# A hybrid retention and attention step on one core: first two units by token pieces, merge exponential before the stores, last down chunk split at token 896

## The chip, the core and the metric

The kernel runs on one core of a Trainium2 chip. The metric is the device time of one execution in microseconds (us), the median of several runs. Engines are named as in the profile: PE (TensorE matmul), PEld (its weight loads), DVE (VectorE), ACT (ScalarE), POOL (GpSimd) and SP (SyncE, which here only issues DMAs).

## What is computed

One inference step for 1024 prompt tokens and 8 sample tokens, 1032 in all, with a model width of 1024. Cut to what matters here:

```python
hn = rms_norm(x, norm_mix)
proj = hn @ w_in                      # rq, rk, rv, rg, aq, ak, av, gate_r, gate_a
ro = swish_gated(group_norm(retention(rq, rk, rv)))
outs, lses = three_dilated_attention_groups(aq, ak, av)
wgt = softmax(stack(lses), axis=0)    # the merge: three groups by their denominators
ao = einsum('gnth,gnthd->nthd', wgt, stack(outs))
merged = sigmoid(gate_r) * (ro @ w_ret) + sigmoid(gate_a) * (ao @ w_att)
x = x + merged @ w_out
hn = rms_norm(x, norm_ffn)
gate, up = split(hn @ w_gate_up)
x = x + (silu(gate) * up) @ w_down
y = rms_norm(x, norm_final)
```

Everything is float32. States, window buffers and new key/value rows are outputs too.

## The kernel before, in words

**Operands.** A product in float32 is made of three passes over operands that are split into a high part and a remainder: high weight by `a_hi`, high weight by `a_lo`, low weight by `a_hi`. All tokens lie transposed in `wide` (128 partitions, 8 rows of k, 1032 tokens); ACT makes `a_hi`, DVE makes `a_lo`. POOL splits each weight tile of `w_raw` into `w_part` with two instructions (L776, L778).

**Units.** A unit is one 128-column tile of a projection over all tokens: 8 steps of k, 3 passes, 3 pieces of 344 tokens, so 72 matmuls into `unit_ps[0]` or `unit_ps[1]`. `unit()` issues them (L896), and its argument `between` puts small tasks (transposes, attention tiles, sums) between the steps of k. A unit waits for its split weights (`w_split`) and until DVE has taken the unit two before from the same PSUM tile (`unit_free`). Splitting the weights of unit j waits until unit j-2 is done. Small tasks use the two banks `task_banks`; `task_done` and `task_free` hand them over. The order on every engine is written out by hand: each engine has one in-order stream.

**Head.** SP loads nine row tiles of x through a ring of four buffers (L543). PE transposes each, four 128x128 blocks to a bank (L934); DVE copies bank 0 and ACT bank 1 into `wide` (L1851, L1353). ACT squares each tile as well (L1361) for the norm. After the ninth tile ACT makes eight whole rows of `a_hi` (L1369), DVE eight of `a_lo` (L1860), and unit 0 follows the rows of `a_lo` as they come. ACT takes the square roots (L1372), DVE the reciprocals and a diagonal matrix `diag` (L1864 to L1869), and `x_norm(j)`, four small PE tasks (L943), spreads the factors over partitions. They stand before steps 0 to 3 of unit 1, and the first waits for `diag_ready`. DVE multiplies by `rstd` as it takes each unit (L1835).

**Merge.** Sixteen branch units begin at `U_BRANCH`; I call them branch unit 0, 1 and so on. `LATE_AT` places fourteen small tasks in them: entry j is (unit, step of k). Entries 0 to 5 and 10 to 13 are sample tasks, entries 6 to 9 the four merge tasks, which transpose `ao_tok` (L1184). `ao_tok` comes out of DVE: `merge_weights` (L2153 to L2173, with ACT's exponential L1627 in its middle), then `merge_group(0)`, `gated_branch(0)`, `merge_group(1)`, `gated_branch(1)`, `merge_group(2)`. Groups 1 and 2 are two 128x2048 instructions each (L2184, L2187). `gated_branch(m)` empties the PSUM tile of branch unit m (L2206).

**Tail.** The last chunk of the down projection runs twice over its 8 output tiles: `last_unit` for token pieces 0 and 1 (688 tokens, 8 x 42 matmuls of 344 columns, L1302), then for piece 2 (8 x 21). Between the latter, `turn_rows(t)` turns finished tiles of 128 tokens back into rows (L1311); ACT squares and takes the root (L1807, L1810), DVE scales (L2437), SP stores. `EARLY` = 688 makes five of nine tiles turn between units, and four after the last one.

Of the kernel before, what the change touches and what calls it, by code (L numbers as in the profile page):

```python
# [29 lines left out]
ALU = mybir.AluOpType  # L30
# [49 lines left out]
EARLY = 2 * PIECE  # L80
# [39 lines left out]
X_ROWS = 4  # L120
# [3 lines left out]
LATE_AT = ((0, 1), (0, 2), (0, 4), (0, 5), (0, 6), (0, 7), (2, 6), (2, 7), (3, 1), (3, 2), (4, 6), (5, 2), (5, 4), (5, 6))  # L124
# [114 lines left out]
def build(nc, a, out):  # L239
    ctx = ExitStack()  # L240
    with ctx:
# [31 lines left out]
        with ExitStack() as s:  # L273
            x_row = sb("x_row", [P, X_ROWS, D], stack=s)
# [113 lines left out]
        x_loaded = [sem(f"x_loaded{i}") for i in range(X_ROWS)]  # L388
# [4 lines left out]
        diag_ready = sem("diag_ready")  # L393
        a_high = sem("a_high")
# [134 lines left out]
        def _(sp):  # L529
# [5 lines left out]
            cols = (COL_RV, COL_RV + P, COL_RK, COL_RQ)  # L535
            for t in range(CHUNKS + 1):
                r = t % X_ROWS
                if t >= X_ROWS:

                    sp.wait_ge(task_done[1], t - X_ROWS + 1)  # L540
                    sp.wait_ge(squared, t - X_ROWS + 1)
                if t < CHUNKS:
                    sp.dma_start(x_row[:, r, :], a["x_prompt"][0, t * P:(t + 1) * P, :]).then_inc(x_loaded[r], 16)  # L543
                else:
                    sp.dma_start(x_row[0:SAMPLES, r, :], a["x_sample"][:, 0, :]).then_inc(x_loaded[r], 16)
                if t == X_ROWS:
                    load(Place(0), 0, KT, w_in[:, :, cols[0]:cols[0] + P])
            for j in range(1, 4):
                load(Place(0), j, KT, w_in[:, :, cols[j]:cols[j] + P])
# [328 lines left out]
        def _(pe):  # L878
# [48 lines left out]
            for t in range(CHUNKS + 1):  # L927
                rows = P if t < CHUNKS else SAMPLES
                pe.wait_ge(x_loaded[t % X_ROWS], 16 * (t // X_ROWS + 1))
                for b in range(2):  # L930
                    ps = begin(Place(0), 2 * t + b)
                    for q in range(4):
                        c = (4 * b + q) * P
                        mm = pe.transpose(ps[:, q * P:q * P + rows], x_row[0:rows, t % X_ROWS, c:c + P], ident[0:rows, 0:rows])  # L934
# [355 lines left out]
            def last_unit(pl, m, taken, ready=None):  # L1290

                s, nf = m % 2, FF_CHUNKS[LAST]
                hi, lo = h_rows(LAST)
                weights = w_part[:, m] if m < 2 else w_keep[:, m - 2]
                pe.wait_ge(w_split, U_LAST + m + 1)
                pe.wait_ge(unit_free[s], pl.half(m))
                for k in range(nf):
                    if ready:
                        pe.wait_ge(ready[0], ready[1] + k + 1)
                    for part, (w, x) in enumerate(((0, hi), (0, lo), (1, hi))):  # L1300
                        for n in taken:
                            mm = pe.matmul(unit_ps[s][:, n, 0:PIECE], weights[:, w, k, :], x[:, k, n * PIECE:(n + 1) * PIECE],  # L1302
                                           start=(k == 0 and part == 0), stop=(k == nf - 1 and part == 2))
                mm.then_inc(unit_done, 1)
# [25 lines left out]
        def _(act):  # L1330
# [24 lines left out]

            for t in range(CHUNKS + 1):
# [8 lines left out]
            for b in range(2):  # L1365
                act.wait_ge(task_free[b], CHUNKS + 1)
            act.wait_ge(gains_loaded, 16)
            for k in range(KT):
                act.activation(a_hi[:, k, :], wide[:, k, :], ACT.Copy, scale=gains[:, 0, k:k + 1]).then_inc(a_high, 1)  # L1369
# [256 lines left out]
            act.wait_ge(mrg_dve, 1)  # L1626
            act.activation(mrg[:, 0:3, :], mrg[:, 0:3, :], ACT.Exp).then_inc(mrg_act, 1)  # L1627
# [187 lines left out]
        def _(dve):  # L1815
# [33 lines left out]
            for t in range(CHUNKS + 1):  # L1849
                n = P if t < CHUNKS else SAMPLES  # L1850
                empty(dve.tensor_copy(wide[:, 0:4, t * P:t * P + n],  # L1851
                                      full(Place(0), 2 * t)[:].rearrange("p (q t) -> p q t", q=4)[:, :, 0:n]), 0)

            dve.wait_ge(const_loaded, 16)
            dve.wait_ge(gains_loaded, 16)
            for b in range(2):
                dve.wait_ge(task_free[b], CHUNKS + 1)
            for k in range(KT):
                dve.wait_ge(a_high, k + 1)
                dve.scalar_tensor_tensor(out=a_lo[:, k, :], in0=wide[:, k, :], scalar=gains[:, 0, k:k + 1],  # L1860
                                         in1=a_hi[:, k, :].bitcast(F32), op0=ALU.mult, op1=ALU.subtract).then_inc(a_ready, 1)

            dve.wait_ge(x_root, 2)
# [560 lines left out]
            for m in range(KT):  # L2424
                ps = take(Place(U_LAST), m)
                x = wide[:, m, 0:EARLY].rearrange("p (n t) -> p n t", t=PIECE)
                dve.tensor_tensor(x, ps[:, 0:2, :], x, ALU.add).then_inc(unit_free[m % 2], 1)
# [14 lines left out]
            for m in range(KT):  # L2442
                ps = take(Place(U_REST), m)
                x = wide[:, m, EARLY:TOKENS]
                dve.tensor_tensor(x, ps[:, 2, :], x, ALU.add).then_inc(unit_free[m % 2], 1)
# [35 lines left out]
```

## Time and profile before

| | us |
|---|---|
| median of 3 runs (range) | 1802.99 (1802.93 to 1804.11) |
| the profiled execution's own time | 1802.53 |
| its span in the profile | 1800.6 |
| mean granted clock of TensorE | 0.995 |
| PE busy | 1769.1 (98%) |
| POOL, DVE, ACT busy | 882.4, 765.8, 473.3 |
| DMA moved | 186.64 MB, 104 GB/s |

The page counts a matmul as busy until its modelled end, and lists time that no engine is seen to need as "issue". Line numbers are those of the kernel before. The granted clock is 1.00 at TensorE's 2.4 GHz and 0.50 at 1.2 GHz.

### The profile page before, as it was taken

The numbers are of one execution on the slowest core, as the hardware profiler recorded it, in microseconds if no ns is written. First come the engines' busy times: TensorE is split into PE (matmuls) and PEld (weight loads), VectorE is DVE, ScalarE is ACT, GpSimd is POOL, SyncE is SP. The second block draws the span as 40 slices with busy tenths as digits, with TensorE's granted clock in tenths as the row PEclk, the third lists the DMA queues.
The fourth block names the chain that finished last, engine by engine and source line by source line (L and its number), as shares of the span: only waits on it lengthen the run. The fifth ranks groups of instructions, "written<-read, shape, count | busy, mean of one in ns | idle before, by whom it ended". The sixth has DMA issues, their size and how long they took to land.

```text
span 1800.6 us, 29667 instructions
## 1 busy us (share of the span) xinstructions
PE 1769.1 (98%) x12218; PEld 1729.1 (96%) x12218; DVE 765.8 (43%) x813; ACT 473.3 (26%) x879; POOL 882.4 (49%) x450
## 2 busy tenths in 40 slices
PE   7999999999999999999899998999999999999998
PEld 6999999999999999999899998999999999999998
DVE  4143444443222213314845678455444444632313
ACT  5001010100411125447101125433333333201003
POOL 3323232324333333332336448988888887344550
PEclk9999999999999999999999999999999999999999
DMA  6212121224222252452834342222222221723122
GB/s 241 83 57 64 57 63 58 66 92 152 82 84 90 76 177 88 150 180 75 236 86 144 126 141 83 71 70 70 92 95 70 93 70 50 291 91 122 53 63 95
DMA packets 172694, 186.64 MB, mean 104 GB/s; under 512 B 7353, under 2 KB 149937, under 8 KB 172633
## 3 DMA queue, kind: packets, MB, share of 16 engines
q1 hardware_dynamic: 143088, 136.87, 23.7%
q10 hardware_dynamic: 29545, 48.90, 7.9%
q8 instruction: 45, 0.74, 0.2%
q14 instruction: 16, 0.13, 0.0%
HBM read 131.99 MB, written 53.76 MB: 103 GB/s over the span
## 4 chain that ended last, share of the span: by engine, by line
PE 92%; DVE 4%; ACT 1%; issue 1%; POOL 1%; DMA 0%; ACTq 0%; DVEq 0%; SPq 0%
PE unit_ps L896 55%; PE pair_ps L1232 23%; PE unit_ps L1302 4%; PE task_banks L1081 2%; PE task_banks L1058 1%; PE task_banks L1068 1%; PE task_banks L1008 1%; PE task_banks L985 1%; PE task_banks L992 1%; PE task_banks L994 1%; PE task_banks L1043 0%; PE task_banks L980 0%; PE task_banks L1016 0%; PE task_banks L965 0%; DVE parts L2184 0%
## 5 line engine op out<-in xcount | busy, mean ns | idle before, releaser
L896 PE MATMUL unit_ps<-a_hi,w_part 128*128 128x344 f32 x3552 | 716.5, 327 | 4.7 <-DVE a_lo L1860 3.7
L896 PEld LDWEIGHTS unit_ps<-a_hi,w_part 128*128 128x128 f32 x3552 | 578.5, 189 | 14.8 <-issue 10.6
L776 POOL TENSOR_TENSOR w_part<-w_raw,consts 128x1024 fp32r<-128x1024 f32 (+1 forms) x89 | 212.2, 2384 | 735.1 <-PE unit_ps L896 705.4
L896 PE MATMUL unit_ps<-a_lo,w_part 128*128 128x344 f32 x1776 | 377.3, 321 | 0.0
L896 PEld LDWEIGHTS unit_ps<-a_lo,w_part 128*128 128x128 f32 x1776 | 300.6, 189 | 0.0
L778 POOL TENSOR_TENSOR w_part<-w_raw,w_part 128x1024 fp32r<-128x1024 f32 (+1 forms) x91 | 240.5, 2643 | 7.0
L1232 PE MATMUL pair_ps<-a_hi,slots_a 128*128 128x258 f32 x1056 | 178.4, 283 | 3.4 <-DVE a_lo L2256 1.5
L1232 PEld LDWEIGHTS pair_ps<-a_hi,slots_a 128*128 128x128 f32 x1056 | 148.8, 190 | 4.5 <-DVE a_lo L2256 1.8
L1835 DVE TENSOR_TENSOR stage<-unit_ps,rstd 128x1032 f32<-128x1032 f32 x42 | 51.7, 1231 | 206.4 <-PE unit_ps L896 206.4
L896 PE MATMUL unit_ps<-b_hi,w_part 128*128 128x344 f32 x720 | 133.4, 320 | 0.0
L896 PEld LDWEIGHTS unit_ps<-b_hi,w_part 128*128 128x128 f32 x720 | 117.0, 188 | 0.3 <-DVE gate_a L2218 0.3
L1232 PE MATMUL pair_ps<-a_lo,slots_b 128*128 128x258 f32 x528 | 96.1, 284 | 1.3 <-issue 1.3
L1715 ACT ACTIVATE snap<-pair_ps 128x516 f32<-128x516 f32 x88 | 52.9, 601 | 143.7 <-PE pair_ps L1232 143.7
L2282 DVE TENSOR_TENSOR h_out<-pair_ps,snap 128x516 f32<-128x516 f32 x44 | 30.5, 694 | 133.2 <-ACT snap L1715 86.5
L1232 PEld LDWEIGHTS pair_ps<-a_lo,slots_b 128*128 128x128 f32 x528 | 77.5, 190 | 1.5 <-issue 1.5
L896 PE MATMUL unit_ps<-b_lo,w_part 128*128 128x344 f32 x360 | 76.2, 320 | 0.0
L830 POOL TENSOR_TENSOR slots_b<-mixed,slots_b 128x512 fp32r<-128x512 f32 x44 | 59.1, 1345 | 24.9 <-ACT slots_b L1706 24.9
L1232 PE MATMUL pair_ps<-a_lo,slots_a 128*128 128x258 f32 x352 | 71.2, 284 | 0.0
L1232 PE MATMUL pair_ps<-s_lo,slots_b 128*128 128x258 f32 x352 | 71.1, 283 | 0.0
L1232 PE MATMUL pair_ps<-s_lo,slots_a 128*128 128x258 f32 x352 | 70.6, 282 | 0.0
L2282 DVE TENSOR_TENSOR temp<-pair_ps,snap 128x516 f32<-128x516 f32 x44 | 30.4, 694 | 86.8 <-ACT snap L1715 46.6
L830 POOL TENSOR_TENSOR slots_a<-mixed,slots_a 128x512 fp32r<-128x512 f32 x44 | 57.5, 1306 | 13.2 <-ACT slots_a L1706 13.2
(266 smaller groups left out, 2677.6 us busy)
## 6 DMA issues: line engine op xcount, KB each, us to landing
w_raw<-in_w_in SPq DMA_DIRECT2D x58, 512.0 KB, 3.9
h_spill<-h_out SPq DMA_DIRECT2D x11, 1032.0 KB, 4.9
raw_a<-in_w_gate_up SPq DMA_DIRECT2D x11, 1024.0 KB, 6.9
raw_b<-in_w_gate_up SPq DMA_DIRECT2D x11, 1024.0 KB, 5.1
att_spill<-stage ACTq DMA_DIRECT2D x18, 516.0 KB, 2.7
att_in<-att_spill ACTq DMA_DIRECT2D x3, 3072.0 KB, 11.5
gate_spill<-stage ACTq DMA_DIRECT2D x16, 516.0 KB, 3.5
a_lo<-h_spill SPq DMA_DIRECT2D x15, 516.0 KB, 5.7
```

The lines of the kernel that those rows point to most:

```text
L776: pool.tensor_tensor(part[:, 0], raw, one, ALU.mult).then_inc(w_high, 1)
L778: pool.tensor_tensor(part[:, 1], raw, part[:, 0].bitcast(F32), ALU.subtract).then_inc(w_split, 1)
L830: pool.tensor_tensor(part_slot(s)[:, 1], source(s, raw), part_slot(s)[:, 0].bitcast(F32), ALU.subtract).then_inc(part_split, 1)
L896: mm = pe.matmul(unit_ps[s][:, n, 0:PIECE], w_part[:, slot, w, k0 + by * k, :], x[:, k, n * PIECE:(n + 1) * PIECE], start=(k == 0 and part ...
L985: mm = pe.matmul(ps[:, q * DV:(q + 1) * DV], k_tok[:, n, :], v_tok[:, n, :], start=True, stop=True)
L992: mm = pe.matmul(ps[:, q * DV:(q + 1) * DV], scores_t[:, n, :], v_tok[:, n, :], start=True, stop=n == 0)
L1081: mm = pe.matmul(ps[:, at:at + HD], probs_t[:, buf, e, blk, :], v, start=(x == 0), stop=(x == len(blocks) - 1))
L1232: mm = pe.matmul(ps[:, n, 0:QUAD], part_slot(s)[:, w, k, :], a[:, n * QUAD:(n + 1) * QUAD], start=(k == 0 and part == 0 and not more), sto ...
L1302: mm = pe.matmul(unit_ps[s][:, n, 0:PIECE], weights[:, w, k, :], x[:, k, n * PIECE:(n + 1) * PIECE], start=(k == 0 and part == 0), stop=(k ...
L1715: act.activation(halves(snap[:, i, :]), ps[:, :, 0:QUAD], ACT.Copy).then_inc(snap_done, 1)
L1835: ins = dve.tensor_tensor(pieces(dst), ps, pieces(rstd[:]), ALU.mult)
L2282: dve.tensor_tensor(halves(out[:, b, h]), ps[:, :, 0:QUAD], halves(snap[:, i, :]), ALU.add).then_inc(combined, 1)
```

## The change

It has three parts.

**Head.** Two weight tiles are loaded first, then all nine tiles of x into nine buffers. Three tiles of x are transposed, then units 0 and 1 run in the order piece 0 of unit 0, piece 0 of unit 1, piece 1 of unit 0 and so on, 24 matmuls a piece, with the other six tiles' transposes at the places in `X_TURN`. ACT and DVE make `a_hi` and `a_lo` in thirds of rows by `X_STEPS`. The squares stand behind all of that on ACT, and `x_norm` moves from unit 1 to unit 2. DVE copies units 0 and 1 out unscaled and multiplies by `rstd` later.

**Merge.** ACT's exponential is issued before the four stores of the sample rows, and the merge tasks move from (2,6), (2,7), (3,1), (3,2) to (3,1), (3,2), (3,4), (3,5).

**Tail.** Token pieces of the last chunk are 448, 448 and 136 wide; `EARLY` becomes 896, `EARLY_TILES` 7.

```diff
-EARLY = 2 * PIECE
+EARLY_PIECE = 448
+EARLY = 2 * EARLY_PIECE
...
-X_ROWS = 4
+X_TURN = {(0, 0, 3): 3, (0, 1, 0): 4, (0, 1, 4): 5, (1, 0, 1): 6, (1, 0, 5): 7, (1, 1, 1): 8}
+
+X_STEPS = (("turn", 0), ("turn", 1), ("turn", 2), ("rows", 0, 0), ("turn", 3), ("rows", 0, 4), ("turn", 4), ("turn", 5),
+           ("rows", 1, 0), ("turn", 6), ("rows", 1, 4), ("turn", 7), ("turn", 8), ("rows", 2, 0), ("rows", 2, 4))
...
-LATE_AT = ((0, 1), (0, 2), (0, 4), (0, 5), (0, 6), (0, 7), (2, 6), (2, 7), (3, 1), (3, 2), (4, 6), (5, 2), (5, 4), (5, 6))
+LATE_AT = ((0, 1), (0, 2), (0, 4), (0, 5), (0, 6), (0, 7), (3, 1), (3, 2), (3, 4), (3, 5), (4, 6), (5, 2), (5, 4), (5, 6))
...
+            for j in range(2):
+                load(Place(0), j, KT, w_in[:, :, cols[j]:cols[j] + P])
             for t in range(CHUNKS + 1):
...
-            unit(Place(0), 0, KT, a_hi, a_lo, ready=(a_ready, 0))
-            unit(Place(0), 1, KT, a_hi, a_lo, between=lambda k: x_norm(k) if k < len(X_NORM) else None)
-            for j in range(2, 4):
-                unit(Place(0), j, KT, a_hi, a_lo)
+            for t in range(3):
+                turn_x(t)
+            for n in range(PIECES):
+                for j in range(2):
+                    pe.wait_ge(w_split, j + 1)
+                    c = slice(n * PIECE, (n + 1) * PIECE)
+                    for k in range(KT):
+                        if (n, j, k) in X_TURN:
+                            turn_x(X_TURN[n, j, k])
+                        if n < PIECES - 1:
+                            pe.wait_ge(a_early, n * KT + k + 1)
+                        else:
+                            pe.wait_ge(a_ready, k + 1)
+                        for part, (w, x) in enumerate(((0, a_hi), (0, a_lo), (1, a_hi))):
+                            mm = pe.matmul(unit_ps[j][:, n, 0:PIECE], w_part[:, j, w, k, :], x[:, k, c],
+                                           start=(k == 0 and part == 0), stop=(k == KT - 1 and part == 2))
+                    if n == PIECES - 1:
+                        mm.then_inc(unit_done, 1)
+
+            unit(Place(0), 2, KT, a_hi, a_lo, between=lambda k: x_norm(k) if k < len(X_NORM) else None)
+            unit(Place(0), 3, KT, a_hi, a_lo)
...
+            act.wait_ge(gains_loaded, 16)
+            for step, *at in X_STEPS:
+                if step == "turn":
+                    turned(*at)
+                else:
+                    rows_high(*at)
             for t in range(CHUNKS + 1):
                 n = P if t < CHUNKS else SAMPLES
-                act.wait_ge(x_loaded[t % X_ROWS], 16 * (t // X_ROWS + 1))
+                act.wait_ge(x_loaded[t], 16)
 
                 wait(act, squared, t)
-                act.activation(x_square[0:n, :], x_row[0:n, t % X_ROWS, :], ACT.Square, accum_out=x_factor[0:n, t:t + 1])\
+                act.activation(x_square[0:n, :], x_row[0:n, t, :], ACT.Square, accum_out=x_factor[0:n, t:t + 1])\
                    .then_inc(squared, 1)
-                turned(t)
...
+            act.wait_ge(mrg_dve, 1)
+            act.activation(mrg[:, 0:3, :], mrg[:, 0:3, :], ACT.Exp).then_inc(mrg_act, 1)
             for b in range(2):
                 act.wait_ge(task_free[b], pl.half(4 + b) + 1)
...
-            act.wait_ge(mrg_dve, 1)
-            act.activation(mrg[:, 0:3, :], mrg[:, 0:3, :], ACT.Exp).then_inc(mrg_act, 1)
...
+            unscaled(0)
             dve.wait_ge(x_root, 2)
...
+            unscaled(1)
             for b in range(2):
                 dve.wait_ge(task_free[b], T_RET // 2)
-
-            scaled(Place(0), 0, v_t[:, 0, :])
-            scaled(Place(0), 1, v_t[:, 1, :])
+            for j in range(2):
+                dve.wait_ge(unit_free[j], 1)
+                step(dve.tensor_tensor(v_t[:, j, :], v_t[:, j, :], rstd[:], ALU.mult))
```

The order on ACT in the head, from the last tile of x to the square roots. Before:

```order
L1361 ACTIVATE x_square,x_factor<-x_row 8x1024 [waits squared,x_loaded0]
L1353 ACTIVATE wide<-task_banks 128x4x8 [waits task_done1]
L1369 ACTIVATE a_hi<-wide,gains 128x1032 [waits gains_loaded,task_free1,task_free0]
L1369 ACTIVATE a_hi<-wide,gains 128x1032 x7
L1372 ACT_TABLE_LOAD
L1372 ACTIVATE x_factor<-x_factor,consts 128x8 [waits squared]
```

And in the change (L1378 is the copy of a tile, L1387 `a_hi`, L1401 the square, L1405 the roots):

```order
L1378 ACTIVATE wide<-task_banks 128x4x8 [waits task_done1]
L1387 ACTIVATE a_hi<-wide,gains 128x344 [waits task_free1,task_free0]
L1387 ACTIVATE a_hi<-wide,gains 128x344 x3
L1387 ACTIVATE a_hi<-wide,gains 128x344 [waits task_free1,task_free0]
L1387 ACTIVATE a_hi<-wide,gains 128x344 x3
L1401 ACTIVATE x_square,x_factor<-x_row 128x1024 [waits x_loaded0]
L1401 ACTIVATE x_square,x_factor<-x_row 128x1024 [waits squared,x_loaded1]
L1401 ACTIVATE x_square,x_factor<-x_row 128x1024 [waits squared,x_loaded2]
```

All nine squares now stand between the last copy and the square roots; before, eight stood ahead of it.

PE from the end of unit 1 into unit 2 in the change (L965 are units 0 and 1, L948 `x_norm`, L898 `unit`):

```order
L965 MATMUL unit_ps<-a_lo,w_part 128x344
L965 MATMUL unit_ps<-a_hi,w_part 128x344
L948 MATMUL task_banks<-diag,consts 128x128 x3
L898 MATMUL unit_ps<-a_hi,w_part 128x344 x3
L898 MATMUL unit_ps<-a_lo,w_part 128x344 x3
```

The first norm task, which waits for `diag_ready`, stands ahead of every matmul of unit 2.

PE at the first two merge tasks in the change (L1206 is the merge transpose), in branch unit 3:

```order
L898 MATMUL unit_ps<-a_hi,w_part 128x344 x3
L1206 MATMUL task_banks<-consts,ao_tok 128x128 x4
L898 MATMUL unit_ps<-a_hi,w_part 128x344 x3
L898 MATMUL unit_ps<-a_lo,w_part 128x344 x3
L898 MATMUL unit_ps<-a_hi,w_part 128x344 x3
L1206 MATMUL task_banks<-consts,ao_tok 128x128 x4
```

The same rows stood three steps of k earlier before, at steps 6 and 7 of branch unit 2.

## Rows read from the trace of the kernel before

**Rows 1.** Page, part 1: PE's busy time over the span
```profile
PE 1769.1 (98%) x12218; PEld 1729.1 (96%) x12218; DVE 765.8 (43%) x813; ACT 473.3 (26%) x879; POOL 882.4 (49%) x450
```

**Rows 2.** PE's waits over the span: us in total, times, longest
```profile
PE task_banks L1184 <- DVE ao_tok L2187: 5.5, 1, 5.5
PE unit_ps L896 <- DVE wide L2206: 0.6, 1, 0.6
```

**Rows 3.** Head, all engines: start us, us, engine line op [idle before <-releaser]
```profile
1.67 1.28 ACT L1361 ACT_TABLE_LOAD   x1 [1.67 <-PEq L2466]
5.23 1.06 ACT L1361 ACTIVATE x_square<-x_row 128x1024 f32<-128x1024 f32 x1 [2.28 <-DMA x_row<-in_x_prompt]
...
5.43 7.24 PE L934 MATMUL task_banks<-consts,x_row 128*128 128x128 f32 x32 [5.43 <-DMA consts<-in_c_small]
```

**Rows 4.** ACT alone at the sixth tile
```profile
14.89 1.06 ACT L1361 ACTIVATE x_square<-x_row 128x1024 f32<-128x1024 f32 x1
...
15.93 0.60 ACT L1353 ACTIVATE wide<-task_banks 128x512 f32<-128x512 f32 x1
```

**Rows 5.** Head, all engines, from the rows of a to the diagonal
```profile
20.73 8.48 ACT L1369 ACTIVATE a_hi<-wide,gains 128x1032 fp32r<-128x1032 f32 x8
...
30.52 0.48 ACT L1372 ACTIVATE x_factor<-x_factor,consts 128x8 f32<-128x8 f32 x2
...
34.18 1.20 DVE L1869 TENSOR_TENSOR diag<-consts,x_factor 128x1024 f32<-128x1024 f32 x1
```

**Rows 6.** Stretches: PE, PEld, DVE, ACT, POOL busy, granted clock, DMA share, GB/s
```profile
20.00:21.00 1.00, 0.04 (x1) 0.00 (x0) 0.00 (x0) 0.92 (x4) 1.00 (x1) 1.00 0.99 291
22.00:28.00 6.00, 4.22 (x13) 3.81 (x14) 5.99 (x4) 6.00 (x6) 3.47 (x2) 0.50 0.14 33
...
893.00:898.00 5.00, 4.80 (x19) 4.74 (x20) 1.74 (x4) 0.00 (x0) 0.00 (x0) 0.50 1.11 315
```

**Rows 7.** Critical chain, norm tasks in unit 1: start us, us, what
```profile
37.74 0.67 PE task_banks L943 x6
...
44.07 21.97 PE unit_ps L896 x138
```

**Rows 8.** DVE alone, taking unit 2
```profile
62.83 1.23 DVE L1835 TENSOR_TENSOR k_t<-unit_ps,rstd 128x1032 f32<-128x1032 f32 x1 [8.86 <-PE unit_ps L896]
```

**Rows 9.** Critical chain around the merge
```profile
865.59 0.38 ACT s_qkv L1614
...
868.98 0.29 ACT mrg L1627
...
869.30 2.70 DVE mrg L2165 x3
...
878.85 4.10 DVE parts L2184
...
888.53 2.30 DVE parts L2184
...
893.20 1.12 PE task_banks L1184 x4
...
903.50 11.50 PE unit_ps L896 x73
```

**Rows 10.** Critical chain: pair stage, last down stage, end
```profile
1115.04 385.04 PE pair_ps L1232 x3196
...
1705.35 56.13 PE unit_ps L1302 x357
1761.48 0.87 PE unit_ps L1311 x8
1762.35 3.31 PE unit_ps L1302 x21
...
1792.24 1.12 ACT y_square L1807 x2
...
1793.78 1.12 ACT y_square L1807 x2
```

More of the change, by code:

```diff
@@ L387, in build @@
         table_loaded = sem("table_loaded")
-        x_loaded = [sem(f"x_loaded{i}") for i in range(X_ROWS)]
+        x_loaded = [sem(f"x_loaded{t}") for t in range(CHUNKS + 1)]
         x_spilled = sem("x_spilled")
@@ L535, in _ @@
             cols = (COL_RV, COL_RV + P, COL_RK, COL_RQ)
+            for j in range(2):
+                load(Place(0), j, KT, w_in[:, :, cols[j]:cols[j] + P])
             for t in range(CHUNKS + 1):
[L537 to L541, printed above, removed]
                 if t < CHUNKS:
-                    sp.dma_start(x_row[:, r, :], a["x_prompt"][0, t * P:(t + 1) * P, :]).then_inc(x_loaded[r], 16)
+                    sp.dma_start(x_row[:, t, :], a["x_prompt"][0, t * P:(t + 1) * P, :]).then_inc(x_loaded[t], 16)
                 else:
[L545 to L548, printed above, removed]
+                    sp.dma_start(x_row[0:SAMPLES, t, :], a["x_sample"][:, 0, :]).then_inc(x_loaded[t], 16)
+            for j in range(2, 4):
                 load(Place(0), j, KT, w_in[:, :, cols[j]:cols[j] + P])
@@ L926, in _, with turn_x @@
             pe.wait_ge(const_loaded, 16)
-            for t in range(CHUNKS + 1):
+            def turn_x(t):
                 rows = P if t < CHUNKS else SAMPLES
-                pe.wait_ge(x_loaded[t % X_ROWS], 16 * (t // X_ROWS + 1))
+                pe.wait_ge(x_loaded[t], 16)
                 for b in range(2):
@@ L1290, in last_unit @@
             def last_unit(pl, m, taken, ready=None):
+                columns = [slice(n * EARLY_PIECE, min((n + 1) * EARLY_PIECE, TOKENS)) for n in range(PIECES)]
                 s, nf = m % 2, FF_CHUNKS[LAST]
@@ L1301, in last_unit @@
                         for n in taken:
-                            mm = pe.matmul(unit_ps[s][:, n, 0:PIECE], weights[:, w, k, :], x[:, k, n * PIECE:(n + 1) * PIECE],
+                            c = columns[n]
+                            mm = pe.matmul(unit_ps[s][:, n, 0:c.stop - c.start], weights[:, w, k, :], x[:, k, c],
                                            start=(k == 0 and part == 0), stop=(k == nf - 1 and part == 2))
@@ L1846, in norm_factor, with turned @@
                 dve.reciprocal(own, own).then_inc(rstd_ready, 1)
-            for t in range(CHUNKS + 1):
+            def turned(t):
                 n = P if t < CHUNKS else SAMPLES
@@ L1852, in _, with rows_low, unscaled @@
                                       full(Place(0), 2 * t)[:].rearrange("p (q t) -> p q t", q=4)[:, :, 0:n]), 0)
+            def rows_low(n, k0):
+                for b in range(2):
+                    dve.wait_ge(task_free[b], 3 * (n + 1))
+                c = slice(n * PIECE, (n + 1) * PIECE)
+                for k in range(k0, k0 + 4):
+                    if n < PIECES - 1:
+                        dve.wait_ge(a_early_high, n * KT + k + 1)
+                    else:
+                        dve.wait_ge(a_high, k + 1)
+                    dve.scalar_tensor_tensor(out=a_lo[:, k, c], in0=wide[:, k, c], scalar=gains[:, 0, k:k + 1],
+                                             in1=a_hi[:, k, c].bitcast(F32), op0=ALU.mult, op1=ALU.subtract)\
+                       .then_inc(a_early if n < PIECES - 1 else a_ready, 1)
             dve.wait_ge(const_loaded, 16)
             dve.wait_ge(gains_loaded, 16)
[L1856 to L1861, printed above, removed]
+            for what, *at in X_STEPS:
+                if what == "turn":
+                    turned(*at)
+                else:
+                    rows_low(*at)
+            def unscaled(j):
+                dve.tensor_copy(pieces(v_t[:, j, :]), take(Place(0), j)).then_inc(unit_free[j], 1)
+            unscaled(0)
             dve.wait_ge(x_root, 2)
```

29 lines of the change are left out of this document (17 added, 12 removed).

## The prediction

> **What bounds the kernel now.** I read the page's busy times first. PE is busy for 1769.1 us of the 1800.6 [rows 1], so almost nothing beside PE's own stream counts: a change pays only where PE stands still, where it runs at the lower clock, or where its instructions get cheaper. The waits of PE came second. The longest wait inside the program is the one for `ao_tok`, 5.5 us, with a small one of 0.64 us for a PSUM tile just before it [rows 2]. Third came the timeline of the head, fourth the critical chain around the merge and at the end. By the stretches, TensorE is granted 0.50 (1.2 GHz) in two places, after PE stood still before unit 0 and after the merge wait, and 1.00 otherwise [rows 6]. So each long wait is paid twice: in itself, and in matmuls at half pace behind it. The two stretches and the tail are what the change touches. In the last stage 357 matmuls of 344 columns take 56.13 us, 0.157 us each [rows 10], which is my price for a matmul; a step of k in a unit (nine) is 1.42 us, a unit 11.3 us.
>
> **Head, what it gives.** The first tile of x had landed when ACT squared it at 5.23 [rows 3]. Now two weight tiles, 1.05 MB, stand ahead of it. At 291 GB/s, the rate while weights alone were loaded [rows 6], that is 3.6 us, so x begins at about 8.8. Four tiles were transposed in 7.24 us [rows 3], 1.8 each; three take until 14.2. ACT's table load of 1.28 us [rows 3] was free while nothing had landed. With the copy as its first instruction it now stands behind the first finished transposes, +1.3. The last copy of a tile is 0.6 [rows 4]. A third of a row of `a_hi` is 8.48/8/3 = 0.35 [rows 5], and `a_lo` about 0.5. The first matmul of unit 0 then comes near 17.0. From there PE has 48 steps of three matmuls, 0.47 each, 22.7 us, and five and a quarter tiles of transposes at 0.87 [rows 10], 4.6 us: 44.3 if it never waits. I add 3.2 for two things: DVE and ACT make a third of a row in about the time PE uses one, and copy tiles between, and part of this runs at the lower clock, as the first steps of unit 0 did before [rows 6]. Units 0 and 1 end at 47.5. Bounds 44.3 and 50.
>
> **Head, the wait it adds.** Before, eight of nine squares were done before the rows of `a_hi`. Now all nine come last. The transposes of the ninth tile stand 23 steps of 0.47 before the end of unit 1, at 47.5 - 10.9 = 36.6. From there ACT needs 0.9 for the copy, 2.8 for eight thirds of rows, and nine squares. A square and the reading of its sum last 1.04 (15.93 - 14.89) [rows 4]; each now waits for the one before, so I take 1.15, together 10.3. The roots are a table load and 0.48 [rows 5], 1.8 together. DVE's reciprocals and `diag` are 1.7, of which 1.20 is one instruction [rows 5], and POOL's splits may hold it 0.7. That is 18.2, so `diag` is ready at 54.8, and PE, whose stream has the first norm task ahead of all of unit 2, stands from 47.5 to 54.8: **a new wait of 7.3 us**. The late split of unit 2's weights (it waits for unit 0, which now ends one piece before unit 1) lies inside this wait; without it it would show by itself. Queued behind PE's wait is everything; behind DVE's wait for the roots are unit 1's copy and the release of its PSUM tile, which unit 3 needs only 13 us later. SP's later loads wait for `rstd`, and have two units of cover.
>
> The norm tasks themselves only move: 44.07 - 37.74 less three steps is 2.1 us [rows 7] in either unit. A wait of 7.3 is longer than the merge wait, after which the clock was 0.50, so I expect half pace again: 2.0 us, between 0 and 3.4 as bounds. Unit 2 ends at 54.8 + 11.3 + 2.1 + 2.0 = 70.2. Before, DVE took it at 62.83 [rows 8], so it ended at 62.5. **Head: +7.7**, with bounds +4 and +11. The Trainium skill (TensorE: Matmul & The Clock Gate, Part 1: The HAM clock gate) says that the switching points depend on a phase that differs from run to run; the traces here hold one run, so I can't check that.
>
> **Merge.** The exponential could start when ACT ended its last copy, 865.59 + 0.38, and starts at 868.98 behind four DMA issues [rows 9]. It comes 3.0 us earlier. DVE's small steps behind it then run before POOL's split at 869.3, while three of them took 2.70 beside it [rows 9]. A large DVE instruction takes 2.30 alone and 4.10 beside POOL [rows 9], as if the two took turns. I count DVE's new chain as 2.0 for the weights, five large instructions of 2.3 and two PSUM takes of 1.25 from 866.3 on, 882.3, plus three of POOL's turns of 2.4: `ao_tok` is ready at 889.5. Branch unit 0's PSUM tile is released early enough that the 0.64 wait goes. Branch unit 3 begins at about 889.6 and reaches its step 1 at 891.0, so the merge tasks don't wait, by 1.5 us. What goes is 5.5 + 0.64, and the half pace behind it: from 893.20 to 903.50 lie 16 transposes and 36 matmuls in 10.3 us [rows 9], which at full pace are 16 x 0.109 + 36 x 0.157 = 7.4. Together 9.0. What is late next: DVE finishes the merge tasks two steps later relative to PE, so the sample scores behind them reach PE's task (4,6) about 0.8 late. The stores of the sample rows come 0.3 us later and nobody waits for them then. **Merge: -8.2**, bounds -9 and -5.
>
> **Tail.** 385.04 us for 3196 matmuls of 258 columns is 0.1205 each [rows 10]; from 258 to 344 columns a column costs 0.00043 us. 448 columns are then 0.2016, and 336 of them instead of 0.157 cost +14.9. For 136 columns no row exists. On the same line they would be 0.068; as the nearest short instruction, the transposes of 128 float32 columns, 0.87/8 = 0.109 [rows 10]. I take 0.075, near the line, since float32 moves more than these operands do per column; keep both ends. 8 x 21 at 0.075 are 12.6, where eight stretches of 3.31 were 26.5 [rows 10]: -13.9. After the last unit two tiles fewer are scaled, 1.54 each by ACT's squares (1793.78 - 1792.24) [rows 10], and the last take is shorter, 0.1: -3.2. **Tail: -2.2**, bounds -3.3 and +3.5. DVE and ACT need at most 2.0 us a tile, less than a short unit and a turn, 2.4. The Trainium skill (TensorE: Matmul & The Clock Gate, Back-to-back issue gap) gives 81 ns between pairs of weight load and matmul at 128 columns; with 0.081, an estimate from that page, the short units are 13.6 and the tail -1.2. No run here shows it yet.
>
> **The sum.** 7.7 - 8.2 - 2.2 = -2.7 against the profiled execution's 1802.53: 1799.8. The median of the runs was 0.5 higher, so I predict 1800.3. A measurement of this kernel can tell about 0.2%, 3.6 us, from no change; this is less.
>
> **Rivals.**
> - *The head's wait is short.* If PE's first pieces are slowed more than ACT's stream, or the clock stays up over the wait, the wait shrinks or costs only itself. For: every hold-up of PE behind the ninth tile's transposes, by a late row of `a_lo` or by half pace, is time that ACT's squares use and the wait doesn't show. Against: ACT has 18.2 us of work after the last tile and PE 10.9, both in fixed order. With +3.5 for the head the time is 1796.1. Chance 0.22.
> - *Weight loads set the pace of the short matmuls.* Each of them still loads 128x128 weights. If the pair costs 0.12 instead of 0.075, the short units gain 7.6 less, and the time is 1807.9: slower than before. It decides from 0.113, where the sum is +3.7. For: the transposes at 0.109 load as many weights. Against: the line through 258 and 344 columns leaves only 0.011 us beside the columns. Chance 0.12. The Trainium skill (the same page, LDWEIGHTS) gives 107 ns for 128 columns of weights; by that, an estimate from the page, the short units are 18.0 and the time 1805.7.
> - *The merge is still late.* If POOL's turns push `ao_tok` by 3 us more, the merge tasks wait 1.5 us again, and if PE's clock falls as well the merge gives 4 us less: 1804.3. Chance 0.08.
> - *All pieces come through at once* and no wait for `diag` is seen, so that the reordering does as its form suggests: head -2, time 1790.6. Chance 0.03.
> - The forecast has the remaining 0.55.
>
> **Numbers.** The forecast itself spans about 1796.5 to 1804. With the first rival and most of the third, and part of the second, the range is 1795.0 to 1807.0. Faster by over 0.2% (below 1799.4): 0.22 + 0.03 and a fifth of the forecast's, 0.11, makes 0.36. Slower by over 0.2% (above 1806.6): 0.11 of the weight-load rival, 0.05 for the head near its upper bound: 0.16. Within: 0.48.
>
> **What the profile after would show.** PE waits for `diag` for about 7 us near 48 to 55, and the granted clock is 0.50 behind it; ACT is busy without a gap from 37 to 53. No PE wait for `ao_tok`; branch units 2 and 3 last 11.3 us apart from their tasks. The last stage's long units take 8.5 us each, the short ones 1.6. The forecast is wrong if the wait for `diag` is under 4 us, if the short matmuls are spaced by over 0.1, or if PE still waits at L1206.

## The result: slower by half a per cent

The changed kernel takes 1813.21 us (median of 5 runs, 1809.62 to 1814.66), the kernel before 1802.93 us beside it: a ratio of 1.0053, with a 95% interval of 1.0043 to 1.0064. By the ratio that is 9.6 us slower (the medians lie 10.3 apart), outside the range 1795.0 to 1807.0, and on the side to which I gave 0.16. The profiled execution is the slowest of the five, 1814.66 us with a span of 1812.7, so what I read from the traces adds up to +12.1 and not to 9.6.

Busy time rose where the work didn't. The page's first part, after (the number of matmuls is that of [rows 1]):

```profile
PE 1775.7 (98%) x12218; PEld 1731.9 (96%) x12218; DVE 772.7 (43%) x831; ACT 478.0 (26%) x895; POOL 882.1 (49%) x450
```

The waits of PE after (us in total, times, longest). The wait for `ao_tok` [rows 2] is gone. The head has a new one, for `diag`. The first transposes stand for x until 9.46, where before they stood for the constants until 5.43. The waits for rows of `a_lo` are not dearer in sum: 3.9 us in four, where before they were 3.7 in two.

```profile
PE task_banks L938 <- DMA x_row<-in_x_prompt: 9.5, 1, 9.5
PE task_banks L948 <- DVE diag L1920: 7.8, 1, 7.8
PE unit_ps L965 <- DVE a_lo L1898: 3.9, 4, 2.2
...
PE task_banks L1177 <- DVE s_score L2144: 1.0, 1, 1.0
```

I read where the time went from the same landmarks in both traces:

| Landmark | before | after | shift |
|---|---|---|---|
| DVE takes unit 2 | 62.83 | 76.11 | +13.3 |
| ACT's last copy of sample rows | 865.59 | 878.88 | +13.3 |
| sample scores leave PE, `s_prob` | 920.74 | 926.02 | +5.3 |
| last down chunk starts | 1705.35 | 1711.26 | +5.9 |
| end of the span | 1800.6 | 1812.7 | +12.1 |

So the head costs 13.3 us, the merge gives 8.0, and the tail costs 6.2. Another 0.6 is lost between the sample scores and the last chunk, where nothing was changed.

**The head after.** The timeline, all engines: start us, us, engine line op out<-in [idle before <-releaser].

```profile
9.46 3.15 PE L938 MATMUL task_banks<-consts,x_row 128*128 128x128 f32 x12 [9.46 <-DMA x_row<-in_x_prompt]
...
11.49 1.28 ACT L1378 ACT_TABLE_LOAD   x1 [11.49 <-PE task_banks L938]
...
17.08 2.00 ACT L1387 ACTIVATE a_hi<-wide,gains 128x344 fp32r<-128x344 f32 x4
17.79 2.04 DVE L1898 SCALAR_TENSOR_TENSOR a_lo<-wide,gains,a_hi 128x344 fp32r<-128x344 f32 x4 [1.66 <-ACT a_hi L1387]
18.52 0.62 PE L965 MATMUL unit_ps<-a_hi,w_part 128*128 128x344 f32 x1 [2.16 <-DVE a_lo L1898]
```

ACT alone, from the last third of `a_hi` to the roots. Nine squares in a chain, each 1.24 us behind the last (rows of the middle ones left out):

```profile
40.83 3.90 ACT L1387 ACTIVATE a_hi<-wide,gains 128x344 fp32r<-128x344 f32 x8
44.63 1.04 ACT L1401 ACTIVATE x_square<-x_row 128x1024 f32<-128x1024 f32 x1
45.58 0.19 ACT L1401 ACTIVATION_READ_ACCUMULATOR x_square<-x_row 128x1 f32 x1
45.86 1.06 ACT L1401 ACTIVATE x_square<-x_row 128x1024 f32<-128x1024 f32 x1
...
55.72 1.28 ACT L1405 ACT_TABLE_LOAD   x1
57.01 0.48 ACT L1405 ACTIVATE x_factor<-x_factor,consts 128x8 f32<-128x8 f32 x2
```

`diag` is ready at 59.1, and PE stands from 51.55 to 59.39. Stretches of after (PE, PEld, DVE, ACT, POOL busy, granted clock, DMA share, GB/s): PE stands still over all of 52 to 58, and from 58 to 65 it works at 0.50.

```profile
52.00:58.00 6.00, 0.00 (x0) 0.00 (x0) 0.43 (x4) 5.21 (x9) 5.38 (x3) 0.76 0.01 3
58.00:65.00 7.00, 5.61 (x23) 5.64 (x24) 2.28 (x3) 0.58 (x2) 0.00 (x0) 0.50 0.01 2
```

**The merge after.** DVE alone: the exponential is out of the way (ACT runs it at 879.15, right behind its last copy), `ao_tok` is complete at 901.18, and PE comes for it at 904.40 without waiting, 3.2 us later. Long instructions beside POOL's take 3.24 and 4.38 by turns, where one alone takes 2.29.

```profile
881.23 2.29 DVE L2234 TENSOR_TENSOR ao_tok<-parts,mrg 128x2048 f32<-128x2048 f32 x1
...
893.52 3.24 DVE L2236 TENSOR_TENSOR parts<-parts,mrg 128x2048 f32<-128x2048 f32 x1
896.80 4.38 DVE L2239 TENSOR_TENSOR ao_tok<-ao_tok,parts 128x2048 f32<-128x2048 f32 x1
```

**The tail after.** The critical chain (start us, us, what), the answer to [rows 10]. 21 short matmuls take 2.30 us, 0.1095 each. Less 21 of these, the 357 leave 68.43 us for 336 long ones, 0.2037 each.

```profile
1711.26 70.73 PE unit_ps L1327 x357
1781.99 0.89 PE unit_ps L1336 x8
1782.89 2.30 PE unit_ps L1327 x21
```

### The profile page after: what moved, and what is told of

It reads as the page before. It is cut to its first block, busy times and chain, and to the rows that moved or that the text cites. A ratio compares the mean times of both kernels' runs of the same rounds, so it can differ in the third digit from the quotient of the medians.

```text
span 1812.7 us, 29711 instructions
## 1 busy us (share of the span) xinstructions
PE 1775.7 (98%) x12218; PEld 1731.9 (96%) x12218; DVE 772.7 (43%) x831; ACT 478.0 (26%) x895; POOL 882.1 (49%) x450
## 4 chain that ended last, share of the span: by engine, by line
PE 91%; DVE 3%; issue 1%; ACT 1%; POOL 1%; DMA 0%; ACTq 0%; DVEq 0%; SPq 0%
PE unit_ps L898 53%; PE pair_ps L1254 22%; PE unit_ps L1327 5%; PE task_banks L1103 2%; PE task_banks L1080 1%; PE task_banks L1090 1%; PE task_banks L1030 1%; PE task_banks L1014 1%; PE task_banks L1007 1%; PE task_banks L1016 1%; PE task_banks L1065 0%; PE task_banks L1002 0%; PE task_banks L987 0%; PE task_banks L1038 0%; POOL slots_b L832 0%
## 5 line engine op out<-in xcount | busy, mean ns | idle before, releaser
L898 PE MATMUL unit_ps<-a_hi,w_part 128*128 128x344 f32 x3456 | 696.3, 326 | 0.2 <-DVE a_lo L2308 0.2
L898 PEld LDWEIGHTS unit_ps<-a_hi,w_part 128*128 128x128 f32 x3456 | 561.8, 189 | 9.4 <-issue 6.2
L898 PE MATMUL unit_ps<-a_lo,w_part 128*128 128x344 f32 x1728 | 366.0, 320 | 0.0
L898 PEld LDWEIGHTS unit_ps<-a_lo,w_part 128*128 128x128 f32 x1728 | 291.3, 189 | 0.0
L898 PE MATMUL unit_ps<-b_hi,w_part 128*128 128x344 f32 x720 | 133.4, 320 | 0.0
L898 PEld LDWEIGHTS unit_ps<-b_hi,w_part 128*128 128x128 f32 x720 | 117.0, 188 | 0.3 <-DVE gate_a L2270 0.3
L2334 DVE TENSOR_TENSOR h_out<-pair_ps,snap 128x516 f32<-128x516 f32 x44 | 30.5, 694 | 132.4 <-ACT snap L1748 86.5
L898 PE MATMUL unit_ps<-b_lo,w_part 128*128 128x344 f32 x360 | 76.2, 320 | 0.0
```

What stands on the lines that cost most here:

```text
L898: mm = pe.matmul(unit_ps[s][:, n, 0:PIECE], w_part[:, slot, w, k0 + by * k, :], x[:, k, n * PIECE:(n + 1) * PIECE], start=(k == 0 and part ...
L2334: dve.tensor_tensor(halves(out[:, b, h]), ps[:, :, 0:QUAD], halves(snap[:, i, :]), ALU.add).then_inc(combined, 1)
```

## The experiments

The ratios are all to the kernel before, run on the same chip beside each; us are the ratio times 1802.9, less 1802.9.

| Kernel | ratio, 95% interval | us against before |
|---|---|---|
| the change | 1.0053 [1.0043, 1.0064] | +9.6 |
| merge part alone | 0.9958 [0.9945, 0.9971] | -7.6 |
| head part alone | 1.0066 [1.0053, 1.0079] | +11.9 |
| tail part alone | 1.0040 [1.0027, 1.0053] | +7.2 |
| change, norm tasks later | 1.0021 [1.0012, 1.0030] | +3.8 |
| change, squares in the gaps | 1.0013 [1.0004, 1.0023] | +2.3 |
| change, x first and squares in the gaps | 1.0020 [1.0011, 1.0029] | +3.6 |
| change, 384 columns | 1.0016 [1.0006, 1.0025] | +2.9 |
| change, x first, squares, 384 | 0.9979 [0.9970, 0.9988] | -3.8 |
| before, merge part, 384 | 0.9952 [0.9938, 0.9965] | -8.7 |

### One part of the change at a time

My theory was the ledger above: three parts that add up. The rival was that each part's price depends on where the other parts have moved the clock, the loads and POOL's turns.

The merge part alone, on the kernel before:

```diff
-LATE_AT = ((0, 1), (0, 2), (0, 4), (0, 5), (0, 6), (0, 7), (2, 6), (2, 7), (3, 1), (3, 2), (4, 6), (5, 2), (5, 4), (5, 6))
+LATE_AT = ((0, 1), (0, 2), (0, 4), (0, 5), (0, 6), (0, 7), (3, 1), (3, 2), (3, 4), (3, 5), (4, 6), (5, 2), (5, 4), (5, 6))
...
+            act.wait_ge(mrg_dve, 1)
+            act.activation(mrg[:, 0:3, :], mrg[:, 0:3, :], ACT.Exp).then_inc(mrg_act, 1)
             for b in range(2):
                 act.wait_ge(task_free[b], pl.half(4 + b) + 1)
             act.dma_start(sample_rows.rearrange("a n c -> n a c"), s_qkv[:]).then_inc(rows_written, 16)
...
-            act.wait_ge(mrg_dve, 1)
-            act.activation(mrg[:, 0:3, :], mrg[:, 0:3, :], ACT.Exp).then_inc(mrg_act, 1)
```

> The kernel before with the middle part of the change alone (exponential ahead of the stores, the later transposes). Theory (the ledger read from the two traces: the merge part gave 8.0 us): faster than before by 7.5 to 9, about 1794.5 us, and PE has no wait for ao_tok. Rival (the gain was produced by the shifted head, whose different phase of clock and loads let DVE's chain come through): under 5 us faster, with a wait for ao_tok left.

It took 1794.31 us, with no wait for `ao_tok`. The theory holds.

The head part alone, that is the changed kernel with the other two parts undone:

```diff
-EARLY_PIECE = 448
-EARLY = 2 * EARLY_PIECE
+EARLY = 2 * PIECE
...
             for b in range(2):
                 act.wait_ge(task_free[b], pl.half(4 + b) + 1)
...
+            act.wait_ge(mrg_dve, 1)
+            act.activation(mrg[:, 0:3, :], mrg[:, 0:3, :], ACT.Exp).then_inc(mrg_act, 1)
```

> The kernel before with the first part of the change alone (units 0 and 1 piece by piece). Theory (the ledger: the head costs 13.3 us where 7.7 were forecast): slower than before by 10 to 14, about 1815 us. Rival (part of the 13.3 is absorbed before the end, since PE then waits less at the merge): slower by 5 to 9, with a wait for ao_tok under 3 us instead of 5.5.

It took 1814.82 us, with all of its waits there beside the old one for `ao_tok`, which gave nothing back. PE's waits of this kernel:

```profile
PE task_banks L947 <- DVE diag L1916: 7.9, 1, 7.9
PE task_banks L1205 <- DVE ao_tok L2235: 5.4, 1, 5.4
PE unit_ps L964 <- DVE a_lo L1894: 3.9, 4, 2.2
```

The tail part alone, on the kernel before:

```diff
-EARLY = 2 * PIECE
+EARLY_PIECE = 448
+EARLY = 2 * EARLY_PIECE
...
+                columns = [slice(n * EARLY_PIECE, min((n + 1) * EARLY_PIECE, TOKENS)) for n in range(PIECES)]
```

> The kernel before with the last part of the change alone (448, 448 and 136 tokens). Theory (short matmuls are spaced 0.1095 us whatever the head did): slower than before by 5.5 to 7, about 1809 us, 21 short matmuls of a unit in 2.30 us. Rival (the spacing came from the state that the longer program had by then, its clock above all): the short units take under 1.9 us and the time is within 3 us of before.

It took 1809.68 us. The last chunk's first 357 matmuls take 70.73 us, to the hundredth as in the changed kernel. -7.6 + 11.9 + 7.2 = +11.5, where the whole change is +9.6; each of the four ratios has an interval of some 2 us to either side, so the parts add up as far as these runs can tell.

### The wait for `diag`: two ways to take it away

First, ask for it later. Only the norm tasks move, from steps 0 to 3 of unit 2 to steps 4 to 7:

```diff
-unit(Place(0), 2, KT, a_hi, a_lo, between=lambda k: x_norm(k) if k < len(X_NORM) else None)
+unit(Place(0), 2, KT, a_hi, a_lo, between=lambda k: x_norm(k - 4) if 4 <= k < 8 else None)
```

> The changed kernel with the four norm tasks at steps 4 to 7 of unit 2 instead of 0 to 3. Theory (PE stands 7.8 us for diag because the first norm task is ahead of all of unit 2, and pays half pace behind it): the wait shrinks to about 1.3 us for the split of unit 2's weights and about 0.7 for diag, the half pace goes, and the time falls by 7 to 9.5 us against the changed kernel. Rival (the wait covers POOL's split of unit 2's and unit 3's weights and DVE's release of PSUM, which then show by themselves): the time falls by under 5 us, with waits of 3 us or more for w_split or unit_free.

1806.60 us median, 6.6 under the changed kernel's: just short of the theory's range and outside the rival's. In its profiled execution the mechanism is as told. PE stands 0.5 us for `diag`, 2.1 for POOL's splits of the weights (1.24 of it for those of unit 2, which the prediction said would show by themselves), and the clock stays at 1.00; its last chunk begins at 1701.96, 9.3 earlier than in the changed kernel's profiled execution. Its stretches, same columns as above:

```profile
52.00:58.00 6.00, 5.53 (x36) 5.24 (x34) 1.61 (x5) 4.10 (x8) 4.28 (x2) 1.00 0.00 0
58.00:65.00 7.00, 7.00 (x48) 6.76 (x49) 1.16 (x2) 1.55 (x4) 0.00 (x0) 1.00 0.00 0
```

The medians show less because the runs of one kernel spread: 1803.8 to 1809.9 here, 1809.6 to 1814.7 for the change. One profiled execution against another is good to 3 us or so, no better.

Second, make it earlier. Five of the nine squares go into ACT's gaps, four stay behind the last row:

```diff
+SQUARES = {('rows', 0, 0): (0, 1), ('rows', 0, 4): (2,), ('turn', 4): (3,), ('turn', 7): (4,)}
+SQUARES_BEFORE = 5
...
             for step, *at in X_STEPS:
...
+                for t in SQUARES.get((step, *at), ()):
+                    square(t)
-            for t in range(CHUNKS + 1):
+            for t in range(SQUARES_BEFORE, CHUNKS + 1):
```

> The changed kernel with five of ACT's nine squares put into the gaps between its copies of x, and four left behind the last row. Theory (the wait for diag comes from nine squares in a chain behind the last tile): ACT's roots end near 51.5 us, diag is ready near 53.7, PE waits about 2.3 us instead of 7.8, and with the half pace behind it the time falls by 6 to 9.5 us against the changed kernel. Rival (the squares in the gaps hold up ACT's copies, and PE waits longer for rows of a_lo): units 0 and 1 end 2 us later or more, and the gain is under 5.

1806.13 us, and the wait is 2.6, where 2.3 were forecast. The rows of `a_lo` weren't held up (4.3 us in four waits, 3.9 before). So the price of squares last is 6 to 9 us of the head's 13.3: the wait and the half pace behind it, as forecast. Neither version brings the head back to the old one, though: in this one DVE takes unit 2 at 67.67, in the kernel before at 62.83. I looked for these 4.8 us next.

### The head's rest: x behind the weights

On the version with squares in the gaps (six of them now, the first ahead of every copy), SP's order:

```diff
-            for j in range(2):
-                load(Place(0), j, KT, w_in[:, :, cols[j]:cols[j] + P])
             for t in range(CHUNKS + 1):
+                if t in (1, 3):
+                    load(Place(0), t // 2, KT, w_in[:, :, cols[t // 2]:cols[t // 2] + P])
```

> The changed kernel with SP's loads in the order x0, first weights, x1, x2, second weights, rest of x, and ACT's squares put into its gaps, the first of them ahead of all copies (so that its table is loaded before data land). Theory (x behind 1.05 MB of weights and the table load behind the first transposes cost 4 us or more of the head; the rest of what is lost are waits for thirds of a_lo and half pace): first transposes near 5.4 us, first matmul of unit 0 near 14, PE's wait for diag under 2, and the time 10 to 13 us under the changed kernel, about 1802. Rival (the first weights and their split of 4.7 us on POOL now end last): PE waits for w_split until 16 or later, and the time is no more than 8 us under the changed kernel.

A miss: 1805.99 us, the same as with x behind the weights (1806.13). The first transposes did begin at 5.44 and the table was loaded at 1.67, but the 4 us that the transposes began earlier were 1.1 by the first matmul of unit 0, at 17.29 (18.43 with squares alone). Two things ate the rest. The second tile of x now landed behind a weight tile (PE waited until 8.45). And the first thirds of `a_lo` fell beside POOL's split of the second weights: four took 3.96 us instead of 2.04, and the first let PE go 2.64 us after it began. All engines of this kernel:

```profile
14.43 2.35 POOL L783 TENSOR_TENSOR w_part<-w_raw,w_part 128x1024 fp32r<-128x1024 f32 x1
14.65 3.96 DVE L1908 SCALAR_TENSOR_TENSOR a_lo<-wide,gains,a_hi 128x344 fp32r<-128x344 f32 x4 [2.39 <-ACT a_hi L1390]
...
17.29 0.63 PE L968 MATMUL unit_ps<-a_hi,w_part 128*128 128x344 f32 x1 [4.92 <-DVE a_lo L1908]
```

The same again at `diag`: the roots were done 2.2 us sooner than with squares alone, and a diagonal of 8x8 elements took 2.38 us beside the next split (it takes 0.22 alone), so PE's wait was 2.6 again. What was left, PE's start at `diag` 1.0 us sooner (52.75 against 53.71), went in the lower clock behind it: DVE takes unit 2 at 68.07, with squares alone at 67.67. DVE alone:

```profile
48.99 2.38 DVE L1928 TENSOR_SCALAR diag<-consts,x_factor 8x8 f32<-8x8 f32 x1
51.29 1.20 DVE L1930 TENSOR_TENSOR diag<-consts,x_factor 128x1024 f32<-128x1024 f32 x1
```

The rival had the time right (7.2 us under the changed kernel, where it allowed 8) and the engine, POOL, but the wrong releaser: PE's matmul waited for `a_lo`, not for `w_split`. I can't say from these runs what a piecewise head would give with POOL's splits moved out of DVE's way; it wasn't tried.

### The short matmuls: what is their floor?

Both kernels leave out work, to see what a pair of weight load and matmul is paid by. In the first, the short matmuls cover 64 columns (the down projection of the last 72 tokens is left out):

```diff
-columns = [slice(n * EARLY_PIECE, min((n + 1) * EARLY_PIECE, TOKENS)) for n in range(PIECES)]
+columns = [slice(n * EARLY_PIECE, min((n + 1) * EARLY_PIECE, EARLY + 64)) for n in range(PIECES)]
```

> The changed kernel with the short matmuls of the last stage over 64 columns instead of 136 (the down projection of the last 72 tokens is left out). Theory (each pair of weight load and matmul has a floor of 0.109 us that no shorter matmul gets under): 21 of them still take about 2.3 us. Rival (they are paid by columns, only dearer than the line through 258 and 344 columns says): about 1.1 to 1.3 us.

In the second they keep 136 columns and load 64 of the 128 columns of weights (half the features of the last 136 tokens are left out):

```diff
+                            o = 64 if n == 2 else P
-mm = pe.matmul(unit_ps[s][:, n, 0:c.stop - c.start], weights[:, w, k, :], x[:, k, c],
+mm = pe.matmul(unit_ps[s][0:o, n, 0:c.stop - c.start], weights[:, w, k, 0:o], x[:, k, c],
```

> The changed kernel with only 64 of 128 weight columns in each short matmul of the last stage, still over 136 tokens (half the features of the last 136 tokens are left out). Theory (the floor is the time that the weights take to load, and that goes by their columns): 21 of them take 1.3 to 1.6 us, and the line's 0.069 becomes visible. Rival (the floor is the issue of a pair, whatever it loads): they still take about 2.3 us.

The critical chain of the first: with less than half the columns the 21 matmuls take 2.27 us, 0.108 each, as good as the 2.30 of 136 columns.

```profile
1781.39 0.93 PE unit_ps L1336 x8
1782.32 2.27 PE unit_ps L1327 x21
```

And of the second: 1.34 us, 0.064 each.

```profile
1777.39 1.00 PE unit_ps L1337 x8
1778.39 1.34 PE unit_ps L1328 x21
```

The theory held in both: the floor goes by the columns of weights, 0.108 to 0.1095 us for 128 of them, and with half of them the 136 columns fall to 0.064, beside the 0.068 that my line gave. The line was near and didn't apply. (The second kernel also writes half as many partitions; these runs don't part the two, but the first excludes the columns that move.) The granted clock over 1783 to 1800 was 1.00 in the changed kernel and in the first of these, and 0.94 in the second. By the formula of the Trainium skill (TensorE: Matmul & The Clock Gate, LDWEIGHTS) 128 columns of weights load in 107 ns, and the trace agrees: 108 with 64 moving columns. The 81 ns that the Trainium skill gives for a pair at 128 columns (the same page, Back-to-back issue gap) don't hold for these operands: no pair with 128 columns of weights that I read here went under 108 ns.

### A split above the floor

If the loss is the floor, a split whose short part stays above it should lose nothing and still gain a tile. This gives 384, 384 and 264 tokens, six tiles early:

```diff
-EARLY_PIECE = 448
+EARLY_PIECE = 384
```

> The changed kernel with its last down chunk split at token 768 (384, 384, 264) instead of 896. Theory (a floor at about 230 columns is what the split pays): long matmuls 0.175 us each, 58.8 for 336, short ones 0.123, 20.7 for 168, and six tiles early; against the changed kernel 7 to 8 us faster, about 1805.6 us. Rival (the loss lies in the dependence of short units and transposes, not in the floor): 264-column units are spaced like the 136-column ones beyond their columns, and the gain is under 4 us.

1805.70 us, 7.5 under the changed kernel's median. The critical chain gives (61.38 - 2.53)/336 = 0.175 for a long matmul and 0.121 for one of 264 columns, against the 0.175 and 0.123 expected:

```profile
1709.21 61.38 PE unit_ps L1327 x357
1770.59 0.87 PE unit_ps L1336 x8
1771.46 2.53 PE unit_ps L1327 x21
```

### The best of it

The old head, the merge part, and the split at 384:

> The kernel before with the merge part and the last down chunk at 384, 384 and 264, its head untouched. Theory (parts add up; 384 columns give the tail 1.4 us against 344, from one tile fewer after the last unit): 9 to 10 us faster than before, about 1793. Rival (the merge's gain and the tail's do not add up): under 8 us faster.

1793.49 us, 0.9952 [0.9938, 0.9965]: about 8.7 us under the kernel before, just short of the theory's 9 to 10 and over the rival's 8, and 18 under the changed one by the ratios (the medians lie 19.7 apart). The merge part alone, on another chip, had 0.9958, so by the times what 384 adds is inside the noise. The two traces tell it better: the last chunk begins at 1696.93 with the merge part alone and at 1696.91 here, and the spans end at 1792.1 and 1791.3. That is 0.8 us, where 1.4 was forecast.

The piecewise head with both mendings and 384:

> The changed kernel with both mended: x ahead of weights and squares in the gaps, and 384, 384 and 264 tokens in the last chunk. Theory (a piecewise head without its wait is worth nothing against the head before, since what it starts earlier it pays in held-up rows): within 3 us of the kernel before's head with the merge and 384 (run beside it), 1792 to 1797. Rival (starting unit 0 at 14 instead of 23.4 us shows, now that the wait is gone): 4 us or more faster than that one, 1789 or less.

1799.00 us, 5.5 slower than with the old head, outside the theory's 3 us on the bad side. The traces put all of it in the head: DVE takes unit 2 at 68.38, with the old head at 62.74. So this piecewise head loses also with both mendings. It doesn't show what one without a wait would do, since a wait is left: `diag` is ready at 50.6, but PE still stands 2.4 us, now for POOL's split of unit 2's weights, and its first nine matmuls behind it take 2.58 us, half pace again. The second half of the split, on POOL, and PE's wait:

```profile
49.23 3.55 POOL L783 TENSOR_TENSOR w_part<-w_raw,w_part 128x1024 fp32r<-128x1024 f32 x1
...
52.83 1.27 PE L951 MATMUL task_banks<-diag,consts 128*128 128x128 f32 x6 [2.40 <-POOL w_part L783]
```

That split can't start before unit 0 is done, and unit 0 now ends only one piece ahead of unit 1. It is the term that the prediction said would show by itself without the wait for `diag`. Taking it away, and putting the norm tasks later in this kernel, were not tried.

## Why the prediction was wrong, step by step

Between the forecast of -2.7 and the +12.1 of the profiled execution lie 14.8 us: 8.4 in the tail, 5.6 in the head, 0.2 in the merge and 0.6 between the sample scores and the last chunk. The two steps that failed are the price of a short matmul and the time of the head's pieces.

- **The merge (-8.2 forecast, -8.0 and -7.6 measured) was right**, though its inner clockwork was not. I had `ao_tok` ready at 889.5 of the old time scale, which is 902.8 here; it was ready at 901.2, since POOL's turns added 6.1 us to DVE's long instructions and not 7.2. No wait, no half pace, no second wait but the 1.0 us at the sample scores that I had put at 0.8.
- **The tail failed at one term above all**: "I take 0.075, near the line, since float32 moves more than these operands do per column". That was a reason for choosing between two ends 0.04 us apart, and I had a better one at hand: the transposes at 0.109 [rows 10] load the same 128x128 weights as the short matmuls, and I read no row in which as many are loaded in less. At 168 x (0.1095 - 0.075) this is 5.8 of the 8.4 us by which the tail came out dearer: the eight short units give 8.0 us (26.4 to 18.4), not 13.9. No run shows that float32 costs the transposes more per column. The long matmuls add 0.7 (0.2037 instead of 0.2016). The rest, 1.9, is a term that my sum left out: seven turns of a tile, 0.89 each, now stand between the short units, where five of 0.87 stood. I had counted the two tiles only where they leave the end. With it the sum closes: +15.6 long, -8.0 short, +1.9 turns, -3.3 at the end, together +6.2.
- **The rival had the tail right.** "Weight loads set the pace of the short matmuls", with its turning point at 0.113 for the whole sum, had chance 0.12. Its mechanism is shown by the two kernels that leave out work, and the prediction's own sign (short matmuls spaced by over 0.1) came. The other two signs, a short wait for `diag` and a wait at L1206, did not. At 0.1095 the sum would have been +3.1, not yet slower by over 0.2%: it needed the head's miss as well.
- **The head's mechanism was right and its size wrong, +13.3 instead of +7.7.** The wait for `diag` was 7.8 where 7.3 were forecast, with half pace behind it. That it came so near is in part luck: from the end of the last tile's transposes to `diag` 18.2 were forecast and 18.6 measured (40.5 to 59.1), but the copy took 0.2 instead of 0.9 and POOL held nothing up instead of 0.7, while eight thirds of rows took 3.9 instead of 2.8 and the squares 11.1 instead of 10.3. The 5.6 are in four steps. The first matmul of unit 0 came at 18.5, not 17.0: x landed at 9.46 instead of 8.8, and a third of a row costs 0.50 on ACT and 0.51 on DVE. "8.48/8/3 = 0.35" divided a fixed cost by three along with the columns; an `a_hi` row of 1032 columns costs 1.06, a third of it half of that. Units 0 and 1 took 33.0 us, not 30.5: three waits for `a_lo` inside them, 1.7 us (the fourth, 2.2, stands ahead of the first matmul), and half pace up to 24.0, where 12 matmuls cost 0.13 more each and 8 transposes 1.6 together instead of 0.9; the 3.2 that I had added was too little. I can't split the rest. The wait was 0.5 longer. And unit 2 took 16.5 behind the wait, not 15.4.
- **The first rival, a short wait, was wrong for the reason that I gave against it**: ACT's list behind the last tile (0.2 + 3.9 + 9 x 1.24 + 1.8 = 17.1) is longer than PE's (11.1, to 51.55). What slowed PE ahead of it slowed ACT too, since ACT waits for PE's transposes.
- **The range** allowed for each miss by itself (head near +11, short matmuls at 0.12) but hardly for both, and both came.

## What to carry to other kernels

When a tile is cut into unequal parts, check the shortest part against the floor per instruction before using a line through long ones: here 0.108 to 0.1095 us for the matmuls of 64 and 136 columns with 128 columns of weights, and 0.5 us for a third of a row (128x344) of `a_hi` on ACT or `a_lo` on DVE. Here the nearest instruction in kind (the same weight load) gave the price better than a line through the same operation at other sizes. Cutting work into pieces so that one engine starts sooner pays only if the engines that feed it have time for the pieces' fixed costs; here unit 0 started 4.9 us earlier (18.52 against 23.45), and the first three units were done 13.3 later.

The cheap edit came from the chain of waits: one small exponential moved ahead of four stores, with the four merge tasks asked for later, gave all that this change gives.

## What the runs showed of the hardware

- DVE's and POOL's instructions that work from SBUF alone read as whole-instruction turns in these traces, and the small instruction pays most: 8x8 elements took 2.38 us beside a POOL instruction of 2.37 (x first), 1.15 with squares in the gaps, where they ended with POOL's instruction at 52.3, and 0.22 alone; four thirds of `a_lo` took 3.96 instead of 2.04. It goes the other way too: behind the next DVE instruction of 1.20, POOL's took 3.41 instead of 2.35 (x first).
- The same wait for `diag`, 2.57 and 2.56 us, was followed by the lower clock in one kernel and not in the other: over 52 to 58 the granted clock was 1.00 with squares in the gaps and 0.72 with x first, and the first norm task took 0.91 and 1.62 (both x6). So half pace followed one of two equally long waits; it cost 0.7 us on that task alone. The Trainium skill (TensorE: Matmul & The Clock Gate, Part 1: The HAM clock gate) says that the switching points depend on a phase that differs from run to run; two kernels with equal waits and unequal clocks agree with that, and it may be why the runs of the changed kernel spread over 5 us; no run here shows the phase.
- The granted clock of a stretch can disagree with its matmuls: it reads 1.00 over 18.5 to 24.3 in the changed kernel, where matmuls of 344 columns follow each other at 0.29 us. That is the pace that they have at a granted 0.50 behind the wait for `diag` (nine in 2.58 us at 61.02); from 25.27 on they follow at about 0.16. The stretch, same columns as above: 12 of these matmuls and 8 transposes in 5.48 busy us.

```profile
18.50:24.30 5.80, 5.48 (x20) 5.00 (x20) 2.02 (x4) 1.70 (x5) 0.00 (x0) 1.00 0.52 125
```
